# Expert layers of a 12-layer stack: the experts of the first 16 first keys worked densely from streamed blocks

## The chip, the cores and the metric

One core of one Trainium2 chip runs one program. The metric is the device time of a whole execution in microseconds. All data are float32; products that need float32 accuracy run either as one f32 matmul, which the trace shows as two MATMUL records, or as three products of split halves (fp32r, "hi" and "lo").

## What is computed

The reference is a stack of twelve layers over x of 256 tokens by 1024 columns: four gated FFNs, stick-breaking attention, latent attention, a state-space mixer, window attention with sinks, and twice the pair that this change touches, an expert layer and a gated embedding layer ("ple"). The expert layer, cut to what matters:

```python
h = rmsnorm(x, norm_g)                                   # 256 x 1024
q = (h @ q_w).reshape(T, 8, 2, 128)                      # 8 heads, two half queries
s = einsum('thcd,ckd->thck', q, sub_keys)                # scores on 128 first and 128 second keys
s1, i1 = top_k(s[:, :, 0], 16); s2, i2 = top_k(s[:, :, 1], 16)
best_s, best_pos = top_k(s1[..., :, None] + s2[..., None, :], 16)
idx  = the pair's i1 * 128 + i2                           # one of 16384 experts
gate = softmax(best_s)
a    = einsum('nd,nhkd->nhk', h, u[idx])                  # each expert: a row u and a row v of 1024
out  = einsum('nhk,nhkd->nd', gate * gelu(a), v[idx])
```

Every token picks 16 experts in each of 8 heads, 128 of 16384, and each picked expert is a row of u and a row of v, 8 KB together.

## The kernel before

Tokens lie on the 128 partitions, in two blocks (tb). A **unit** n (0 to 15) is one head of one block; a unit has 16 **picks**, worked in four **groups** of four (the last unit in eight smaller ones, FINE). For one pick GpSimd issues an indirect DMA that brings, for each of the 128 tokens, its row of `experts` (u and v side by side) into one of 11 buffers, `held`. VectorE makes the dot product of u with h (`dots`, L2723, one instruction of 1024 elements), ScalarE takes Gelu, multiplies by the gate and spreads the weight of each token on a diagonal (`weights`: L1903, L1905, L1912), and TensorE adds diagonal times v to the layer's sum in PSUM (`values`: L1300 and L1303, two halves of 512 columns). The last product of a pick frees its buffer (`expert_free`), and GpSimd waits for that before it issues the gather 11 picks later.

Each engine works through its own instruction list in order, and semaphores join the lists. The lists are written out by hand, group by group:

- TensorE, `peer`: 4 queries ahead (a query m is 8 products of a 128x128 weight block with 256 tokens, L1258; its key scores are L1288), then for each group: on every second group `key_scores(m - 1)` and `query(m)`, then `values`. `query_beside` says which query stands in which group; there are 16 of them, two for each head (both blocks at once).
- ScalarE: on those groups `scores(m - 1)` (PSUM to SBUF, L1884), then `weights`, then the copy of query m (L1892), which TensorE's key scores need.
- VectorE: `dots` of a group, and between the groups of unit n the search for unit n + 1: `gates` and `top_keys`, `top_pairs`, `experts_of` (L2665 to L2714 and L2179 to L2190), which yields the indices for the gathers.
- GpSimd: the gathers in order of picks, and some low parts (L401) of the ple layer's weight blocks.
- SP: the queue of the stream. All other weights come as blocks of 128x1024 (512 KB) from `stream`, four in a ring, and a load waits until the block four before it has been used (or split). Queries have places of their own.

In the last four units the ple layer begins beside the values (`ple_beside_values`).

The lines that set the order on TensorE:

```python
for n in range(UNITS):
    for group in range(len(groups_of(n))):
        m = query_beside(n, group)
        if m is not None:
            key_scores(m - 1)
            query(m)
        if m == SUBS - 1:
            key_scores(m)
        values(n, group)
        ple_beside_values(l, n, group)
```

Of the kernel before, what the change touches and what calls it, by code (L numbers as in the profile page):

```python
# [7 lines left out]
U32 = mybir.dt.uint32  # L8
# [33 lines left out]
RING = 4  # L42
LAYERS = ["ffn0", "sb", "ffn1", "ffn2", "mla", "ffn3", "ssm", "peer0", "ple0", "swa", "peer1", "ple1"]
# [3 lines left out]
         ("peer0_q", SUBS), ("ple0_proj", 2), ("ple0_gate", 8),  # L47
         ("swa_kv", 2), ("swa_q", 8), ("swa_out", 8),
         ("peer1_q", SUBS), ("ple1_proj", 2), ("ple1_gate", 8)]
# [29 lines left out]
LATE_BY_DVE = {AT[part] + k for part, ks in (("sb_out", (5, 7)), ("ple0_gate", (5, 7)), ("ple1_gate", (5, 7)),  # L79
# [64 lines left out]
EARLY_GATE = {(PH + 6, 2): 0, (PH + 6, 3): 1, (PH + 7, 0): 2, (PH + 7, 1): 3}  # L144
# [13 lines left out]
def build_program(nc, stream, experts, x_in, pos_in, cols_in, rows_in, out):  # L158
    n_blocks = AT["end"]
    ctx = ExitStack()  # L160
    with ctx:
# [149 lines left out]
        def peer_regions():  # L311
# [3 lines left out]
                       ("pk", (2, TOPK)), ("at", (TOPK,)), ("idx", (2, TOPK)), ("e", (2, TOPK)), ("sum", (1,)),  # L315
                       ("rc", (1,)), ("gate", (2, TOPK)), ("a", (2, TOPK)), ("g", (2, TOPK)), ("w", (2, TOPK)),
                       limit=HELD_AT)
            r["held"], _ = region(HELD_AT, HELD, EXPERT)
# [19 lines left out]
        h_for_queries = plain("h_for_queries", hT_at, KD, T)  # L338

# [43 lines left out]
        def make_hi(act, b, i=None, per_turn=0):  # L383

            wait_loaded(act, b, i, per_turn)
            if b in NEXT_IN_RING:
# [201 lines left out]
        def _(pe):  # L588
# [314 lines left out]
            def mla():  # L903
# [26 lines left out]
                latent_block(3, 0).then_inc(of("mla_first"), 1)  # L930
# [5 lines left out]
                for tb in range(TB):  # L936
# [15 lines left out]
                    if tb == 0:  # L952
                        last.then_inc(of("mla_q_done"), 1)
                for tb in range(TB):
# [10 lines left out]
                    if tb == 0:  # L965
                        last.then_inc(of("mla_kv_done"), 1)
# [127 lines left out]
            def ssm():  # L1094
# [47 lines left out]
                pe.wait_ge(of("ssm_ex"), 1)  # L1142
# [108 lines left out]
            def peer(l):  # L1251
# [41 lines left out]
                def values(n, group):  # L1293
                    tb = n // PH
                    pe.wait_ge(of("peer_diag"), group_count(l, n, group) + 1)
                    for k in range(*groups_of(n)[group]):
                        first, end = n % PH == 0 and k == 0, n % PH == PH - 1 and k == TOPK - 1
# [3 lines left out]
                        if tb == 1 and (first or end):  # L1301
                            lower.then_inc(y_ready, 1)
                        pe.matmul(ps[:, 2 * tb + 1, :], diag, v[:, HALF:D], start=first, stop=end)\  # L1303
                          .then_inc(of("expert_free"), 1)

# [24 lines left out]
            def ple_beside_values(l, n, group):  # L1330
# [11 lines left out]
                if (n, group) == (PH + 5, 0):  # L1342
                    pe.wait_ge(of("ple_pT"), l + 1)
                    project(1, 4).then_inc(of("ple_second"), 1)
                if (n, group) == (PH + 5, 1):
                    project(0, 0)
                if (n, group) == (PH + 5, 2):
# [1679 lines left out]
```

## Time and profile before

| | |
|---|---|
| median of 3 runs | 2742.69 us (2741.33 to 2744.24) |
| span of the profiled execution | 2739.2 us |
| TensorE busy (with modelled ends of matmuls) | 2461.3 us, 90% |
| VectorE busy | 1915.0 us, 70% |
| ScalarE busy | 1178.3 us, 43% |
| GpSimd busy | 855.8 us, 31% |
| gathers | 512, 536.90 MB |
| stream and the rest | 237.45 MB |

Busy shares are means over layers with different limits. How an expert layer stands has to be read from windows cut at its own ends, from who waits for whom there, and from the distances between starts in the timeline, since matmuls overlap their own ends.

### The profile page before, as it was taken

How to read it: one execution, taken by the hardware profiler on the slowest of the kernel's cores; microseconds unless marked ns; L12 is line 12 of the kernel's file. 1: busy time of each engine (PE TensorE's matmuls, PEld its weight loads, DVE VectorE, ACT ScalarE, POOL GpSimd, SP SyncE). 2: the span in 40 equal slices, each digit the busy share in tenths (PEclk: the TensorE clock that was granted, in tenths of full speed). 3: DMA queues.
4: the chain of work that ended last, by engine and by line, in shares of the span. 5: the costliest groups of instructions: out<-in, count | busy, mean ns of one | idle time of the engine just before them, and what ended most of it. 6: DMA issues, size and time to landing. Idle time of an engine off the chain costs nothing.

```text
span 2739.2 us, 32208 instructions
## 1 busy us (share of the span) xinstructions
PE 2461.3 (90%) x10416; PEld 1678.3 (61%) x10416; DVE 1915.0 (70%) x3841; ACT 1178.3 (43%) x2586; POOL 855.8 (31%) x700
## 2 busy tenths in 40 slices
PE   8999999999989999998998787789988998777688
PEld 7888788888778877986544333334765454333244
DVE  7885588888768875654676767666667676776675
ACT  4446744444564456563333333333453333323334
POOL 0005400000230026754333333444433333333442
PEclk9999999999999999999999889999999999999999
DMA  6654365556425553448999999999639999999996
GB/s 209 189 180 139 117 198 190 172 192 190 158 70 195 188 163 127 165 142 331 420 418 421 417 419 415 414 414 420 205 142 413 420 421 421 417 420 417 411 414 265
DMA packets 142240, 783.39 MB, mean 286 GB/s; under 512 B 15904, under 2 KB 16416, under 8 KB 76576
## 3 DMA queue, kind: packets, MB, share of 16 engines
q0 software_dynamic: 73728, 536.90, 47.4%
q1 hardware_dynamic: 65648, 237.45, 26.1%
q10 hardware_dynamic: 2736, 7.46, 0.9%
q8 instruction: 66, 1.08, 0.2%
q14 instruction: 62, 0.51, 0.1%
HBM read 780.69 MB, written 1.05 MB: 285 GB/s over the span
## 4 chain that ended last, share of the span: by engine, by line
PE 48%; DMA 22%; issue 9%; DVE 8%; ACT 7%; POOL 6%; another core or an unknown queue 0%; POOLq 0%; ACTq 0%; SPq 0%; DVEq 0%
DMA arena<-experts,arena 22%; PE ps L717 11%; PE ps L1300 6%; PE ps L1303 6%; PE ps L718 6%; PE ps L695 5%; PE ps L696 5%; PE ps L697 5%; POOL ring_lo L401 4%; DVE arena L2723 2%; ACT row L1912 2%; POOL arena L2840 1%; PE ps L1258 1%; ACT arena L1905 1%; ACT L1903 1%
## 5 line engine op out<-in xcount | busy, mean ns | idle before, releaser
L2723 DVE SCALAR_TENSOR_TENSOR arena<-arena,ps 128x1024 f32<-128x1024 f32 x512 | 616.4, 1219 | 370.3 <-DMA arena<-experts,arena 354.0
L1300 PE MATMUL ps<-arena,row 128*128 128x512 f32 x1024 | 568.3, 638 | 197.3 <-ACT row L1912 190.3
L2840 POOL DMA_INDIRECT arena<-experts,arena x512 | 485.3, 948 | 761.4 <-PE ps L1303 508.9
L1303 PE MATMUL ps<-arena,row 128*128 128x512 f32 x1024 | 549.7, 620 | 0.0
L717 PE MATMUL ps<-hT,ring_hi 128*128 128x512 f32 x1408 | 503.4, 400 | 2.9 <-DVE hT L2239 2.7
L394 ACT ACTIVATE ring_hi<-ring 128x1024 fp32r<-128x1024 f32 x408 | 429.8, 1058 | 172.4 <-PE ps L697 127.4
L1300 PEld LDWEIGHTS ps<-arena,row 128*128 128x128 f32 x1024 | 198.2, 202 | 474.5 <-ACT row L1912 259.5
L401 POOL TENSOR_TENSOR ring_lo<-ring,ring_hi 128x1024 fp32r<-128x1024 f32 x139 | 334.5, 2416 | 235.0 <-ACT ring_hi L394 212.7
L718 PE MATMUL ps<-hT,ring_lo 128*128 128x256 f32 x1408 | 395.9, 281 | 0.0
L1303 PEld LDWEIGHTS ps<-arena,row 128*128 128x128 f32 x1024 | 205.5, 201 | 266.4 <-issue 266.4
L401 DVE TENSOR_TENSOR ring_lo<-ring,ring_hi 128x1024 fp32r<-128x1024 f32 x269 | 324.1, 1228 | 18.3 <-ACT ring_hi L394 17.6
L717 PEld LDWEIGHTS ps<-hT,ring_hi 128*128 128x128 f32 x1408 | 265.3, 188 | 69.7 <-issue 3.1
L2817 POOL TENSOR_TENSOR rs<-ms,cols 128x1 f32<-128x1 f32 (+1 forms) x41 | 26.4, 645 | 842.2 <-DVE ms L2053 733.1
L718 PEld LDWEIGHTS ps<-hT,ring_lo 128*128 128x128 f32 x1408 | 266.7, 189 | 2.8
L1903 ACT ACTIVATE arena<-arena 128x4 f32<-128x4 f32 (+1 forms) x138 | 28.4, 206 | 533.2 <-DVE arena L2723 513.3
L1912 ACT ACTIVATE row<-cols,arena 128x128 f32<-128x128 f32 x512 | 164.6, 390 | 4.5
L695 PE MATMUL ps<-ring_hi,w 128*128 128x512 f32 x352 | 138.3, 393 | 3.0 <-DVE ring_lo L401 3.0
L1542 ACT ACTIVATE arena<-arena 128x256 f32<-128x256 f32 x88 | 36.9, 419 | 235.7 <-DVE arena L2280 235.7
L696 PE MATMUL ps<-ring_lo,w 128*128 128x512 f32 x352 | 137.9, 392 | 0.0
L697 PE MATMUL ps<-ring_hi,w 128*128 128x512 f32 x352 | 137.0, 389 | 0.0
L695 PE MATMUL ps<-hT,ring_hi 128*128 128x256 f32 (+1 forms) x392 | 114.1, 291 | 4.3 <-POOL ring_lo L401 2.4
L1905 ACT ACTIVATE arena<-arena 128x1 f32<-128x1 f32 x512 | 110.2, 284 | 4.5
(350 smaller groups left out, 3599.4 us busy)
## 6 DMA issues: line engine op xcount, KB each, us to landing
ring<-stream SPq DMA_DIRECT2D x424, 512.0 KB
arena<-experts,arena POOLq DMA_INDIRECT x512
row<-rows_in ACTq DMA_DIRECT2D x11, 512.0 KB, 5.2
arena<-stream SPq DMA_DIRECT2D x8, 512.0 KB, 5.8
queries_in_ring_hi<-stream SPq DMA_DIRECT2D x8, 512.0 KB
queries_in_w<-stream SPq DMA_DIRECT2D x4, 512.0 KB, 7.8
queries_in_h_lo<-stream SPq DMA_DIRECT2D x4, 512.0 KB, 5.3
x<-x_in SPq DMA_DIRECT2D x1, 1024.0 KB, 5.3
```

The lines of the kernel that those rows point to most:

```text
L394: act.activation(part(b)[0], raw(b), ACT.Copy).then_inc(hi_ready, 1)
L401: e.tensor_tensor(lo, raw(b), hi.bitcast(F32), ALU.subtract).then_inc(lo_ready[who], 1)
L695: pe.matmul(dst, a[0], b[0], start=start, stop=False)
L696: pe.matmul(dst, a[0], b[1], start=False, stop=False)
L697: return pe.matmul(dst, a[1], b[0], start=False, stop=stop)
L717: pe.matmul(ps[:, bank_at, :], hi, hT[:, :, k, :], start=k == 0, stop=False)
L718: last = pe.matmul(ps[:, bank_at, 0:T], lo, hT_hi[:, k, :], start=False, stop=k == KD - 1)
L1300: lower = pe.matmul(ps[:, 2 * tb, :], diag, v[:, 0:HALF], start=first, stop=end)
L1303: pe.matmul(ps[:, 2 * tb + 1, :], diag, v[:, HALF:D], start=first, stop=end)\
L1912: last = act.activation(R["diag"][:, k % (2 * GROUP), :], col("ident"), ACT.Copy, scale=R["w"][:, n % 2, k:k + 1])
L2723: last = dve.scalar_tensor_tensor(u, u, 1.0, h, ALU.mult, ALU.mult, accum_out=R["a"][:, n % 2, k:k + 1])
L2840: pool.indirect_dma_start(R["held"][:, g % HELD, :], None, experts, bass.IndirectOffsetOnAxis(ap=idx[:, n % 2, k:k + 1], axis=0))\
```

## The change

The keys are numbered 0 to 127, and an expert's index is first key times 128 plus second key. The experts whose first key is below `DENSE` = 16 are the first 2048 of the table. For these, u and v of the layer are laid into the stream: 16 blocks of u (transposed, one block for each first key) and 16 of v for each layer. The rest follows from that:

- **up**: `up(c)` multiplies block c of u with all of h (8 products of 256 tokens), one block in each group from (3, 0) to (6, 3); VectorE multiplies two blocks at a time with the inverse norm (`normed_dense`), ScalarE takes Gelu. The result is 128 second keys x 16 first keys x 256 tokens.
- **gates**: the picks of all 8 heads of a block are turned (`turned_picks`), VectorE compares them with iota (`first_keys_of`, `second_keys_of`), GpSimd multiplies the first-key comparison by the gate (`gated_first_keys`), and for each token one product of 128 picks x 128 second keys with 128 picks x 16 first keys gives the token's gates on all 2048 experts (`dense_gates`, 16 tokens in a "half", 16 halves, in units 8 to 10). VectorE multiplies them in (`dense_weights`).
- **down**: `down(c)` adds weights times block c of v to the same PSUM sums (4 products of 512 columns), from (10, 3) to (12, 3).
- **gathers**: an index whose first key is below 16 gets 2^20 added and falls out of the bounds check, so its row is not fetched (not in unit 0). Its gate in `values` is zero (`masked`), and the value products are made for all picks as before. From unit 2 on `dots` writes its elementwise result elsewhere.
- **order**: queries stand one in each group of units 0 to 2, and behind the values instead of before them. Searches are done two to a unit from unit 2 to 7 (`SEARCHED`). The ple layer's first steps move back by two to four groups; six low parts go from GpSimd to VectorE.
- Elsewhere some semaphores that one engine signals in order are merged into one (FFN, latent attention, state space).

```diff
-            m = FRONT + (len(EVEN) * n + group) // 2
-            return m if group % 2 == 0 and m < SUBS else None
+            m = FRONT + len(EVEN) * n + group
+            return m if m < SUBS else None
...
+SEARCHED = [[1], [2], [3, 4], [5, 6], [7, 8], [9, 10], [11, 12], [13, 14], [15]] + [[] for _ in range(UNITS - 9)]
+GATED_HALVES = {(8, 0): 1, (8, 1): 1, (8, 2): 1, (8, 3): 1, (9, 0): 2, (9, 1): 2,
+                (9, 2): 1, (9, 3): 2, (10, 0): 2, (10, 1): 2, (10, 2): 1}
+DENSE_VALUES = {(10, 3): 2, (11, 0): 2, (11, 1): 2, (11, 2): 2, (11, 3): 1, (12, 0): 2, (12, 1): 2, (12, 2): 2, (12, 3): 1}
+FIRST_KEYS = {(7, 2): 0, (9, 2): 1}
+TURNED_PICKS = {(7, 1): 0, (9, 1): 1}
...
                         if m is not None:
                             key_scores(m - 1)
+                        if (n, group) in TURNED_PICKS:
+                            turned_picks(TURNED_PICKS[n, group])
+                        values(n, group)
+                        if m is not None:
                             query(m)
                         if m == SUBS - 1:
                             key_scores(m)
-                        values(n, group)
+                        dense_beside_values(n, group)
...
+                def up(c):
+                    b, p = AT[f"peer{l}_u"] + c, c // 2
+                    if c % 2 == 0:
+                        if p < 2:
+                            pe.wait_ge(of("peer_s"), n0 + SUBS)
+                        else:
+                            pe.wait_ge(of("dense_by_dve"), by_dve(l, "normed", p - 2))
+                    wait_loaded(pe, b)
+                    for k in range(KD):
+                        last = pe.matmul(dense_bank(p)[:, (c % 2) * T:(c % 2 + 1) * T], raw(b)[:, k * P:(k + 1) * P],
+                                         parts_for_queries(k, slice(0, T)), start=k == 0, stop=k == KD - 1)
+                    last.then_inc(used, 1)
...
+                def dense_gates(i):
+                    pe.wait_ge(of("dense_by_pool"), HALVES // 2 * l + i // 2 + 1)
+                    pe.wait_ge(of("dense_by_dve"), by_dve(l, "second_keys", i))
...
+                    for t in range(TOPK):
+                        last = pe.matmul(gates_in(i)[:, t, :], second_keys[i % 2][:, t, :], first_keys[:, TOPK * i + t, :],
+                                         start=True, stop=True)
...
+                def down(c):
...
+                    for tb in range(TB):
+                        for half in range(2):
+                            last = pe.matmul(ps[:, 2 * tb + half, :], dense[:, c, tb * P:(tb + 1) * P],
+                                             raw(b)[:, half * HALF:(half + 1) * HALF],
+                                             start=False, stop=tb == 0 and c == DENSE - 1)
...
+                def normed_dense(p):
+                    if p == 0:
+                        dve.wait_ge(of("dense_by_act"), by_act(l, "inverse"))
+                    dve.wait_ge(used, AT[f"peer{l}_u"] + 2 * p + 2)
...
+                def dense_beside_dots(n, group):
+                    q = len(EVEN) * n + group - SUBS + FRONT
+                    if q >= 2 and q % 2 == 0 and q < DENSE + 2:
+                        normed_dense((q - 2) // 2)
+                    before = halves_of(*((n, group - 1) if group else (n - 1, len(EVEN) - 1)))
+                    for i in before:
+                        dense_weights(i)
+                    if (n, group) in FIRST_KEYS:
+                        first_keys_of(FIRST_KEYS[n, group])
+                    for i in halves_of(n, group):
+                        second_keys_of(i)
...
+                        dots(n, group)
+                        if group == 0:
+                            for searched in SEARCHED[n - 1] if n else [0]:
+                                gates(searched)
+                        dense_beside_dots(n, group)
+                        for _ in range((2, 1, 2, 1)[group] if len(SEARCHED[n]) > 1 else 1):
+                            if searches:
+                                part_of, searched = searches.pop(0)
+                                part_of(searched)
...
+                        if n:
+                            pool.indirect_dma_start(into, None, experts, rows, bounds_check=2 * KEYS * KEYS - 1,
+                                                    oob_is_err=False).then_inc(expert_landed[g % HELD], 16)
```

ScalarE's order within a group is not touched: `scores(m - 1)`, `weights`, the copy of query m.

## Rows read from the trace of the kernel before

**Rows 1.** The page's head.
```profile
span 2739.2 us, 32208 instructions
```
**Rows 2.** Windows: length, busy PE, PEld, DVE, ACT, POOL (instructions), PEclk, DMA share, GB/s.
```profile
1291.90:1403.50 111.60, 102.83 (x283) 52.97 (x284) 77.64 (x185) 37.48 (x123) 42.30 (x45) 0.97 1.01 421
1403.50:1602.50 199.00, 170.73 (x442) 82.82 (x442) 139.30 (x345) 66.65 (x215) 75.02 (x79) 0.95 1.01 418
1602.50:1801.50 199.00, 154.35 (x311) 64.02 (x310) 137.62 (x343) 61.20 (x190) 77.08 (x80) 0.91 1.01 414
1801.50:1927.40 125.90, 112.78 (x272) 52.02 (x270) 82.75 (x185) 47.71 (x144) 52.90 (x50) 0.95 0.99 411
2077.00:2712.70 635.70, 534.09 (x1305) 249.49 (x1305) 437.17 (x1056) 213.06 (x673) 248.29 (x253) 0.95 1.01 416
1572.70:1574.70 2.00, 2.00 (x3) 0.97 (x4) 1.48 (x5) 0.00 (x0) 0.00 (x0) 0.50 1.06 442
```
**Rows 3.** TensorE's waits in 1291.9 to 1927.4: us in total, times, longest.
```profile
PE ps L1300 <- ACT row L1912: 90.5, 42, 5.6
```
**Rows 4.** Timeline of TensorE: start, length; a value half, key scores, a query, values.
```profile
1304.90 1.02 PE L1303 MATMUL ps<-arena,row 128*128 128x512 f32 x2
1305.76 0.61 PE L1288 MATMUL ps<-arena,pick 128*128 128x128 f32 x4
1306.20 3.62 PE L1258 MATMUL ps<-h_for_queries,ring 128*128 128x256 f32 x16
1309.66 1.02 PE L1300 MATMUL ps<-arena,row 128*128 128x512 f32 x2
```
**Rows 5.** Timeline of TensorE in the state-space layer: f32 products of 64 columns.
```profile
1151.96 1.90 PE L1192 MATMUL ps<-arena 128*128 128x64 f32 x16
1153.69 0.65 PE L1194 MATMUL ps<-arena 128*128 128x256 f32 x2
```
**Rows 6.** Timeline of ScalarE beside rows 4, and a Gelu table load later.
```profile
1306.40 0.63 ACT L1884 ACTIVATE arena<-ps,rs 128x128 f32<-128x128 f32 x2 [8.26 <-PE ps L1288]
1306.92 0.20 ACT L1903 ACTIVATE arena<-arena 128x4 f32<-128x4 f32 x1
...
1308.05 1.28 ACT L1912 ACTIVATE row<-cols,arena 128x128 f32<-128x128 f32 x4
1309.86 0.38 ACT L1892 ACTIVATE pick<-ps 128x256 f32<-128x256 f32 x1 [0.54 <-issue]
...
1568.95 1.28 ACT L1903 ACT_TABLE_LOAD   x1 [7.57 <-DVE arena L2714]
```
**Rows 7.** Timeline of TensorE after an idle time: first value half, fourth.
```profile
1572.70 2.08 PE L1300 MATMUL ps<-arena,row 128*128 128x512 f32 x2 [3.97 <-ACT row L1912]
...
1577.82 1.02 PE L1303 MATMUL ps<-arena,row 128*128 128x512 f32 x2
```
**Rows 8.** Timeline of VectorE: where gates, dots, pairs and experts begin and end.
```profile
1568.24 0.17 DVE L2712 TENSOR_REDUCE arena<-arena 128x1 f32<-128x16 f32 x1
...
1571.65 1.22 DVE L2723 SCALAR_TENSOR_TENSOR arena<-arena,ps 128x1024 f32<-128x1024 f32 x1
...
1572.79 1.22 DVE L2723 SCALAR_TENSOR_TENSOR arena<-arena,ps 128x1024 f32<-128x1024 f32 x1
...
1578.17 0.42 DVE L2698 TENSOR_TENSOR arena<-arena 128x256 f32<-128x256 f32 x1
...
1581.09 1.21 DVE L2723 SCALAR_TENSOR_TENSOR arena<-arena,ps 128x1024 f32<-128x1024 f32 x1
...
1588.12 0.17 DVE L2179 TENSOR_SCALAR arena<-arena 128x16 uint32<-128x16 uint32 x1
...
1591.08 1.21 DVE L2723 SCALAR_TENSOR_TENSOR arena<-arena,ps 128x1024 f32<-128x1024 f32 x1
```
**Rows 9.** Groups of VectorE by shape: a comparison of 512 elements.
```profile
L2185 DVE TENSOR_TENSOR arena<-arena,cols 128x512 f32<-128x512 f32 x15 | 10.4, 692 | 0.5
```
**Rows 10.** The page's groups: a low part on GpSimd, 1024 elements.
```profile
L401 POOL TENSOR_TENSOR ring_lo<-ring,ring_hi 128x1024 fp32r<-128x1024 f32 x139 | 334.5, 2416 | 235.0 <-ACT ring_hi L394 212.7
```

More of the change, by code:

```diff
@@ L1296, in values @@
                     for k in range(*groups_of(n)[group]):
-                        first, end = n % PH == 0 and k == 0, n % PH == PH - 1 and k == TOPK - 1
+                        first, end = n % PH == 0 and k == 0, n == UNITS - 1 and k == TOPK - 1
                         v = R["held"][:, (PICKS * l + TOPK * n + k) % HELD, D:]
@@ L1300, in values @@
                         lower = pe.matmul(ps[:, 2 * tb, :], diag, v[:, 0:HALF], start=first, stop=end)
-                        if tb == 1 and (first or end):
+                        if end:
                             lower.then_inc(y_ready, 1)
@@ L1304, in values, with inverse_row @@
                           .then_inc(of("expert_free"), 1)
+                def inverse_row():
+                    pe.wait_ge(of("dense_by_act"), by_act(l, "spread"))
+                    for b in range(TB):
+                        last = pe.matmul(ps[:, 6, b * P:(b + 1) * P], col("ones"), R["spread"][:, b, :], start=True, stop=True)
+                    last.then_inc(of("dense_by_pe"), 1)
+                def up(c):
[10 more added lines that the diff above has]
+                    last.then_inc(used, 1)
@@ new lines, in down @@
+                def down(c):
+                    b = AT[f"peer{l}_v"] + c
+                    if c == 0:
+                        pe.wait_ge(of("dense_weights"), HALVES * (l + 1))
+                    wait_loaded(pe, b)
+                    for tb in range(TB):
[3 more added lines that the diff above has]
+                                             start=False, stop=tb == 0 and c == DENSE - 1)
+                        if tb == 0 and c == DENSE - 1:
+                            last.then_inc(y_ready, 1)
+                    last.then_inc(used, 1)
@@ new lines, in dense_beside_values @@
+                def dense_beside_values(n, group):
+                    c = dense_up(n, group)
+                    if c is not None:
+                        if c == 0:
+                            inverse_row()
+                        up(c)
+                    for i in halves_of(n, group):
+                        dense_gates(i)
+                    first = begun_at(DENSE_VALUES, (n, group))
+                    for c in range(first, first + DENSE_VALUES.get((n, group), 0)):
+                        down(c)
@@ L1914, in weights, with spread_inverse, inverse_row, gelu @@
                     last.then_inc(of("peer_diag"), 1)
+                def spread_inverse():
+                    act.wait_ge(of("peer_sp"), n0 + SUBS)
+                    for b in range(TB):
+                        last = act.activation(R["spread"][:, b, :], col("ident"), ACT.Copy, scale=rs[:, b:b + 1])
+                    last.then_inc(of("dense_by_act"), 1)
+                def inverse_row():
+                    act.wait_ge(of("dense_by_pe"), by_pe(l, "inverse"))
+                    act.activation(R["inverse"], ps[:, 6, 0:T], ACT.Copy).then_inc(of("dense_by_act"), 1)
+                def gelu(p):
+                    act.wait_ge(of("dense_by_dve"), by_dve(l, "normed", p))
+                    pair = dense[:, 2 * p:2 * p + 2, :]
+                    act.activation(pair, pair, ACT.Gelu).then_inc(of("dense_by_act"), 1)
+                def turned_picks(tb):
+                    act.wait_ge(of("dense_by_pe"), by_pe(l, "turned", tb))
+                    act.activation(R["turned"][:, tb], split(ps[:, 5 if tb else 2, 0:3 * P], 3, P), ACT.Copy)\
+                       .then_inc(of("dense_by_act"), 1)
+                def dense_beside_weights(n, group):
+                    q = len(EVEN) * n + group - SUBS + FRONT
+                    if q == 0:
+                        inverse_row()
+                    if q >= 3 and q % 2 and q < DENSE + 3:
+                        gelu((q - 3) // 2)
+                    if (n, group) in TURNED_PICKS:
+                        turned_picks(TURNED_PICKS[n, group])
                 second_high_parts()
```

266 lines of the change are left out of this document (184 added, 82 removed).

## Prediction

> **What bounds the kernel now.** The span of the profiled execution is 2739.2 us [rows 1]; the median of the runs shown is 2742.69, so what is worked out on the span gets 3.5 us added. I took the page's 40 slices first, saw DMA near full only in the two stretches of the expert layers, and then asked for windows cut at the first and last value product of each layer [rows 2]: 1291.9 to 1927.4 in layer 0 (635.5 us) and 2077.0 to 2712.7 in layer 1 (635.7 us). The four windows of layer 0 hold 48, 80, 80 and 48 picks; the reader should see a DMA share of 0.99 to 1.01 and 411 to 421 GB/s in all of them. The waits say the same: TensorE waited 90.5 us for ScalarE's diagonals [rows 3], which follow VectorE's dots and so the gathers. So one expert row pair of 1.05 MB costs 2.49 us, a unit of 16 picks 39.8 us, and any byte saved there looks like time saved. But TensorE is the next limit and not far off: 541 us of busy time in 635.5 (the first four windows of rows 2 together), with modelled ends in it. Its real pace is in the timeline: one half of a pick's value product every 0.86 us [rows 4], so four picks take 6.86 us of the 9.95 that their gathers take. All that TensorE has left per layer is 635 - 64 x 6.86 = 196 us, of which the 12 queries beside the values (3.46 us each, and 0.44 for the key scores [rows 4]) take 47 and the work of the next layer some 20.
>
> **The change, part by part.**
> Bytes removed: counting in the reference on these inputs, 4022 and 4068 rows of units 1 to 15 have a first key below 16, 66.3 MB at 8 KB a row. Bytes added: 64 blocks of 0.524 MB, 33.6 MB. Net 32.7 MB, 78 us at 417 GB/s, if bytes still decided.
>
> TensorE, added per layer. Up: 16 blocks of the very shape of a query, 16 x 3.46 = 55 us. Down: 16 x 4 products of 512 columns at 0.86, 55 us. Gates: 256 products with 128 weight columns and 16 moving ones. The trace has none. From below: if only moving columns cost, a query's record of 256 columns at 0.216 us gives 0.014 each, 7 us in all. From above: key scores with 128 columns, 4 records in 0.44 us, 56 us. The nearest row has 64 columns: 16 records from 1151.96 to 1153.69, 0.108 each [rows 5]. I take 0.108, thus 0.216 a token, 3.46 for a half of 16 tokens, 55 us in all. (The Trainium skill, TensorE: Matmul & The Clock Gate, section LDWEIGHTS, says that a weight load takes its number of stationary columns divided by 1.2, in ns; for 128 that is 107, and the row agrees. The same page's formula for an isolated gap, section Back-to-back issue gap, goes by moving columns; by it the 512 records would cost some 5 us and TensorE's sum be 624, not 674, an estimate; the page says itself that it under-counts at few columns.) Sum: 165 us added to about 506, 671 and with transposes 674, against 635 before. No value product is taken away: every pick keeps its two halves, with weight zero. That alone turns a saving of bytes into a loss.
>
> Then the order. I call w TensorE's work in a group and follow who waits.
>
> Units 0 to 2 (12 groups). Before, on every second group, TensorE did key scores, query, values, and the query (3.46) hid ScalarE's scores and weights. Now each group does key scores of m-1, values, query m. ScalarE's queue has scores(m-1) ahead of weights of the group, and scores(m-1) need the query that TensorE made at the end of the group before. So a chain stands bare in each group: drain and copy 0.20 + 0.38 (1309.66 to 1310.24), 0.05, key scores to scores 0.64, scores 0.52, Gelu to last diagonal 2.41 (1306.92 to 1309.33), 0.05: 4.25 us [rows 4, 6]. Group = 6.86 + 3.46 + 4.25 = 14.6. Twelve: 175; two Gelu table reloads of 1.28 [rows 6]: 178; and before (3,0) the spread of rs, an Exp load and exponentials, and two units' gates ahead of that Gelu: about 5.3: 183. All of VectorE and the gathers hide under it.
>
> The clock. After an idle of 3.97 us TensorE is granted 0.50, the 1.2 GHz level, and takes 5.12 us (1572.70 to 1577.82) for three halves that take 2.57 at 2.4 GHz [rows 7, 2]. Gaps of 3 to 4 us are what the new chains make, so each may cost 0 to 2.55; the mean grant of 0.91 in the third window says not each one, and I take 1.5. Units 0 to 2: 183 + 12 x 1.5 = 201, before 111.6.
>
> Units 3 to 7. The searches go two to a unit. VectorE's pieces [rows 8]: gates plus keys 3.41 (by its small instructions I give gates 0.5 of it, 0.8 with the new mask, and keys 2.9), pairs 2.92, experts 2.96, a dot 1.14 (four 4.7 with the new wait for the group before). normed_dense(p) stands in VectorE's queue after dots of q = 2p+2 and waits for up(2p+1), which TensorE does after the values of q-1. From its end: 0.2 + 0.69 (512 elements, [rows 9]) + keys and pairs 5.8 + dots 4.7 + ScalarE 2.6 = 14.0 us to the next group's values, while TensorE has values and up, 10.3. So 3.7 idle, plus clock 1.5: a pair of groups 25.8 instead of 19.9. Two free groups 21.2, seven pairs 181, gates of two units three times 1.6: 5; unit 7 is VectorE's (14.0 + 1.6, then 8.7, 12.8 with first_keys, 7.7): 44. Together 250, before 199.
>
> Units 8 to 12. A 2048-element comparison is four of the 0.69 rows less their fixed part, 2.3 us [rows 9]; 16 + 2 a layer, 41 us that VectorE hides except in unit 8, where search and comparison chain with TensorE as above (13.1 against 10.3, 11.7 a group): 48 with clock. Units 9 and 10: 27.4 + 7 and 5 halves of 3.46, 2 downs of 3.43: 51.6 each, and 3 for the wait of turned_picks(1) on dense_weights. Units 11 and 12: 27.4 + 7 x 3.43 = 51.4 each. Sum 257, before 199.
>
> Units 13 to 15: gathers bound again, 16 x 2.49 x 0.87 = 34.6 a unit, with the stream's blocks and the tail 108, before 126.
>
> Costed at nothing, with their cover: GpSimd's multiply of 512 elements (half of a low part's 2.42 us [rows 10]) and a bounds check per gather, both under its idle time, as 79 instructions took 75.02 us of 199 [rows 2], 0.95 each of the 2.49 between gathers; they would show if an issue passed 2.5 us. SP's loads of u and v wait for blocks used, 1.26 us each at 417 GB/s against 3.4 us or more between uses; uncovered, 16 x 1.26 x 2. Low parts moved from GpSimd to VectorE, at most 6 x 2.42, lie in units 13 to 15 where VectorE waits for rows. The merged semaphores in the FFN layers only join counts of one queue. Block 0's sum, mean and power come later, in the same waits.
>
> Layer: 201 + 250 + 257 + 108 = 816 against 635.5, +180.5; two layers +361; 2739.2 + 361 + 3.5 = 3104, say 3100.
>
> **The rivals.**
> A, bytes decide: 2742.7 - 78 = 2665. It needs TensorE's 674 us under 635 - 39 = 596, so values or ups cheaper than rows 4, from the point where w falls under 9.3 us a group. DMA at 1.01 speaks for it, the pace of 0.86 against it. This is the one on the other side of zero.
> B, TensorE alone: the chains are hidden because VectorE and ScalarE run ahead. Units 0 to 2: 3 x 27.4 + 47 = 129; 3 to 6: 4 x 41.3 = 165; 7: 35; 8 to 12: 137 + 110 = 247; 13 to 15: 108. That is 684, +48 a layer, 2840. For it: VectorE is busy for 437 of 635.5 us [rows 2]. Against it: both chains close through a queue's own order, which being ahead can't cure.
> C, dearer: the lower clock takes every stall in full and a checked gather or comparison beside GpSimd costs more: 3104 + 44 x 1.05 = 3150 and beyond, to 3300.
> D, the skipped rows are fetched all the same: 676 us of DMA a layer, under 816, so no change to my number; with B it would still be 2840.
>
> **How the numbers follow.** Forecast 70%, its own range 3030 (no clock loss) to 3160 (2.55 each time). B, or a part of the chains hidden down to 2950: 15%. C above 3200: 8%. A: 5%. No change 2%. If gates cost their low bound, VectorE's chain takes over in units 8 to 10 and 25 us a layer go, to 2980 with no clock loss. The range of 8 in 10 is 2950 to 3200. 0.2% (5.5 us) is what a measurement of this kernel tells from none: faster 0.05, same 0.02, slower 0.93.
>
> **What would show it.** Value products with 14 to 17 us from group to group in units 0 to 2, TensorE idle behind ScalarE's diagonals once for each; in units 3 to 6 idle of some 4 us on every second group and VectorE waiting for L1258's like; gates at 0.108 a record; DMA share near 0.75 over the layer, 1.0 only at its end. Wrong if DMA stays at 1.0 throughout, or if group distances in units 0 to 2 stay near 11.

## The result, and the profile after

The changed kernel takes 3178.91 us (median of 4 runs, 3177.32 to 3180.35) against 2742.01 (4 runs); the ratio is 1.1599, with a 95% interval of 1.1582 to 1.1615. That is slower by 437 us. The prediction said 3100 in 2950 to 3200, and slower with 0.93.

First the page of the changed kernel, the rows that answer to [rows 1] and to the busy times and gathers of the table before.

```profile
span 3177.7 us, 37104 instructions
...
PE 2896.0 (91%) x12228; PEld 2004.9 (63%) x12228; DVE 2027.2 (64%) x3999; ACT 1157.0 (36%) x2588; POOL 878.2 (28%) x704
...
q0 software_dynamic: 73728, 470.66, 39.8%
q1 hardware_dynamic: 74864, 271.00, 25.1%
...
PE 69%; DVE 12%; issue 7%; ACT 6%; POOL 4%; DMA 2%; POOLq 0%; ACTq 0%; SPq 0%; DVEq 0%
```

The reader is to see that the gathers moved 66 MB less (470.66 for 536.90), the stream 34 MB more (271.00 for 237.45), as counted. The last line is the chain that ended last: 69% TensorE and 2% DMA, where it was 48% and 22% before. The saving of bytes came, and in this kernel it was worth nothing: DMA is hardly on that chain any more.

Windows of the changed kernel, layer 0, cut by the count of value records (16 for each group of four picks) at the starts of units 0, 3, 8, 13 and at the end. The columns are those of [rows 2].

```profile
1285.60:1492.50 206.90, 155.80 (x432) 85.84 (x432) 92.41 (x253) 47.91 (x156) 47.24 (x48) 0.87 0.66 241
1492.50:1749.20 256.70, 221.43 (x584) 119.39 (x585) 191.23 (x545) 65.92 (x210) 80.00 (x81) 0.88 0.83 311
1749.20:2043.60 294.40, 284.60 (x964) 166.04 (x962) 149.46 (x239) 50.53 (x186) 91.95 (x88) 0.87 0.78 286
2043.60:2147.10 103.50, 99.27 (x248) 47.56 (x248) 60.42 (x100) 38.52 (x122) 41.63 (x39) 0.96 0.89 355
```

The DMA share is 0.66 to 0.89 where it was 0.99 to 1.01, and the granted clock 0.87 to 0.88 in the first three windows and 0.96 in the last, where it was 0.91 to 0.97. The same cut on the kernel before gives 120.8, 199.8, 205.4 and 109.5 us. The windows of [rows 2] were cut some 9 us early: they do not hold 48 picks in the first, as the prediction said, and the 111.6 and 126 that it compared with should have been 120.8 and 109.5. The layer's sum is not touched by that. Layer 1 after the change is 861.8 us long, layer 0 861.5, before 635.5 and 635.4. So 452 us were added in the layers, and 14 us less lie outside them. The kernels below that are made from the code before with one edit in the expert layer have 12 to 16 us less there too, so these are not the work of the change's edits outside the layers. Ten of the 14 can be placed: shortly before the first values of each layer of the kernel before, TensorE waited 4.67 and 5.33 us for ScalarE's copy of a query, and e9_before_skip shows no wait there. The first of the two:

```profile
1277.22 0.78 PE L1272 MATMUL ps<-arena,pick 128*128 128x128 f32 x2 [4.67 <-ACT pick L1874]
```

Why ScalarE was late there stays open. When a kernel is compared with the kernel before, the layers say what an edit did in them; the medians hold these 14 us as well.

### The profile page after: what moved, and what is told of

It is laid out like the page before. It is cut to its first block, busy times and chain, and to the rows that moved or that the text cites. A ratio compares the mean times of both kernels' runs of the same rounds, so it can differ in the third digit from the quotient of the medians.

```text
span 3177.7 us, 37104 instructions
## 1 busy us (share of the span) xinstructions
PE 2896.0 (91%) x12228; PEld 2004.9 (63%) x12228; DVE 2027.2 (64%) x3999; ACT 1157.0 (36%) x2588; POOL 878.2 (28%) x704
## 3 DMA queue, kind: packets, MB, share of 16 engines
q0 software_dynamic: 73728, 470.66, 39.8%
q1 hardware_dynamic: 74864, 271.00, 25.1%
## 4 chain that ended last, share of the span: by engine, by line
PE 69%; DVE 12%; issue 7%; ACT 6%; POOL 4%; DMA 2%; POOLq 0%; ACTq 0%; SPq 0%; DVEq 0%
PE ps L1371 14%; PE ps L1374 12%; PE ps L788 9%; PE ps L789 5%; PE ps L766 5%; PE ps L767 5%; PE ps L768 5%; PE ps L1416 4%; POOL ring_lo L472 4%; PE ps L1427 3%; PE ps L1329 3%; PE ps L1392 2%; DMA arena<-experts,arena 2%; ACT row L2056 2%; DVE arena L2910 2%
## 5 line engine op out<-in xcount | busy, mean ns | idle before, releaser
L1371 PE MATMUL ps<-arena,row 128*128 128x512 f32 x1024 | 614.7, 686 | 198.1 <-ACT row L2056 197.9
L2910 DVE SCALAR_TENSOR_TENSOR arena<-arena,ps 128x1024 f32<-128x1024 f32 x376 | 448.5, 1217 | 247.5 <-DMA arena<-experts,arena 242.5
L1374 PE MATMUL ps<-arena,row 128*128 128x512 f32 x1024 | 578.6, 649 | 0.0
L1371 PEld LDWEIGHTS ps<-arena,row 128*128 128x128 f32 x1024 | 214.6, 217 | 447.6 <-issue 228.6
L1374 PEld LDWEIGHTS ps<-arena,row 128*128 128x128 f32 x1024 | 219.7, 215 | 294.9 <-issue 294.9
L472 POOL TENSOR_TENSOR ring_lo<-ring,ring_hi 128x1024 fp32r<-128x1024 f32 x127 | 306.0, 2420 | 233.3 <-ACT ring_hi L465 211.5
L472 DVE TENSOR_TENSOR ring_lo<-ring,ring_hi 128x1024 fp32r<-128x1024 f32 x281 | 338.7, 1228 | 18.4 <-ACT ring_hi L465 17.4
L1416 PEld LDWEIGHTS ps<-first_keys,second_keys 128*128 128x128 f32 x1024 | 150.6, 236 | 10.5 <-issue 10.5
L1416 PE MATMUL ps<-first_keys,second_keys 128*128 128x16 f32 x1024 | 148.7, 296 | 0.0
L2910 DVE SCALAR_TENSOR_TENSOR queries_in_h_lo<-arena,ps 128x1024 f32<-128x1024 f32 x96 | 113.6, 1216 | 27.2 <-DMA arena<-experts,arena 27.2
```

The lines of the kernel that those rows point to most:

```text
L472: e.tensor_tensor(lo, raw(b), hi.bitcast(F32), ALU.subtract).then_inc(lo_ready[who], 1)
L1371: lower = pe.matmul(ps[:, 2 * tb, :], diag, v[:, 0:HALF], start=first, stop=end)
L1416: last = pe.matmul(gates_in(i)[:, t, :], second_keys[i % 2][:, t, :], first_keys[:, TOPK * i + t, :], start=True, stop=True)
L2910: last = dve.scalar_tensor_tensor(unread(n, k, u), u, 1.0, h, ALU.mult, ALU.mult, accum_out=R["a"][:, n % 2, k:k + 1])
```

## The experiments

Stage times of layer 0, all counted alike, from the profiled execution of each kernel; the median is that of its runs (e13_before_skip_all has one run):

| kernel | median us | units 0-2 | 3-7 | 8-12 | 13-15 | layer |
|---|---|---|---|---|---|---|
| before | 2742 | 120.8 | 199.8 | 205.4 | 109.5 | 635.4 |
| changed | 3179 | 206.9 | 256.7 | 294.4 | 103.5 | 861.5 |
| e1_query_first | 3013 | 129.9 | 245.0 | 294.4 | 103.6 | 772.9 |
| e2_gates_apart | 3193 | 206.5 | 256.7 | 301.6 | 103.7 | 868.5 |
| e3_filler | 3151 | 191.5 | 254.7 | 294.4 | 104.1 | 844.8 |
| e4_norm_later | 3080 | 206.8 | 209.4 | 290.4 | 103.7 | 810.3 |
| e5_before_new_queries | 2894 | 207.9 | 196.3 | 205.0 | 109.5 | 718.6 |
| e6_gates_mid | 3153 | 206.7 | 256.7 | 281.2 | 104.1 | 848.7 |
| e8_gates_wide | 3119 | 206.8 | 256.7 | 265.1 | 105.0 | 833.6 |
| e9_before_skip | 2673 | 119.9 | 189.6 | 194.5 | 103.8 | 607.9 |
| e10_gates_64_columns | 3126 | 206.4 | 256.7 | 267.9 | 104.3 | 835.3 |
| e11_together | 2869 | 129.9 | 204.6 | 264.3 | 104.2 | 703.0 |
| e12_together_sum_later | 2852 | 129.9 | 206.8 | 259.4 | 105.6 | 701.6 |
| e13_before_skip_all | 2499 | 115.0 | 160.6 | 142.9 | 99.2 | 517.7 |

**Queries ahead of the values again.**

```diff
                             turned_picks(TURNED_PICKS[n, group])
-                        values(n, group)
                         if m is not None:
                             query(m)
                         if m == SUBS - 1:
                             key_scores(m)
+                        values(n, group)
```

> The changed kernel, with query m ahead of the values again (still one in each group of units 0 to 2). If the chain query copy, key scores, scores, weights stands bare because the query comes behind the values, then the query of 3.46 us hides it: a group of units 0 to 2 falls from 17.2 us to 10.8 to 11.2, the stage from 207 to 130 to 140 us, and the kernel to about 3040. If the groups are long for another reason (rows landing late, VectorE), the stage stays above 190 us and the time at 3179.

3012.6 us, ratio 1.099 (1.0972 to 1.1008). One group of the changed kernel in the timeline of TensorE:

```profile
1311.47 3.62 PE L1329 MATMUL ps<-h_for_queries,ring 128*128 128x256 f32 x16
1315.56 0.71 PE L1359 MATMUL ps<-arena,pick 128*128 128x128 f32 x4 [0.47 <-ACT pick L2036]
1319.28 2.07 PE L1371 MATMUL ps<-arena,row 128*128 128x512 f32 x2 [3.00 <-ACT row L2056]
1321.14 1.92 PE L1374 MATMUL ps<-arena,row 128*128 128x512 f32 x2
```

And ScalarE beside it, the same chain as in [rows 6]:

```profile
1315.12 0.38 ACT L2036 ACTIVATE pick<-ps 128x256 f32<-128x256 f32 x1 [12.37 <-PE ps L1329]
1316.31 0.62 ACT L2028 ACTIVATE arena<-ps,rs 128x128 f32<-128x128 f32 x2 [0.80 <-PE ps L1359]
1316.83 0.20 ACT L2047 ACTIVATE arena<-arena 128x4 f32<-128x4 f32 x1
...
1317.95 1.28 ACT L2056 ACTIVATE row<-cols,arena 128x128 f32<-128x128 f32 x4
```

The query ends about 1314.93, the values begin at 1319.28: 4.35 us bare, 4.25 predicted, and then a half takes 1.86 us (1319.28 to 1321.14) for 0.86 at full clock. The kernel's time is 27 us under the expected 3040: the stage is at the low end of 130 to 140, and units 3 to 7 gave another 12 us in layer 0. With the query ahead most groups take 10.8 or 10.9 us, and TensorE in that stage goes from 155.80 busy in 206.90 to 126.81 in 129.90 at clock 1.00:

```profile
1284.80:1414.70 129.90, 126.81 (x416) 74.95 (x416) 92.47 (x253) 47.80 (x157) 46.59 (x47) 1.00 0.94 366
```

**The change's handling of the queries alone, on the kernel before.**

```diff
-            m = FRONT + (len(EVEN) * n + group) // 2
-            return m if group % 2 == 0 and m < SUBS else None
+            m = FRONT + len(EVEN) * n + group
+            return m if m < SUBS else None
...
                             key_scores(m - 1)
+                        values(n, group)
+                        if m is not None:
                             query(m)
                         if m == SUBS - 1:
                             key_scores(m)
-                        values(n, group)
```

> The kernel before with one thing of the change: a query in every group of units 0 to 2, behind the values. By the bare chain the stage takes 207 us instead of 121 and the rest, bound by gathers, is as before: 2742 + 2 x 86 = about 2914. Rival: the harm needs the dense layer's other loads on ScalarE and VectorE, and alone it is below 30 us, 2770.

2893.8 us, ratio 1.056 (1.0542 to 1.0577): 207.9 us in units 0 to 2 with none of the dense work. Its waits there are the changed kernel's: in the first fence the changed kernel, in the second this one.

```profile
PE ps L1371 <- ACT row L2056: 43.0, 12, 5.5
```

```profile
PE ps L1300 <- ACT row L1913: 42.7, 12, 5.3
```

So a good third of the loss is there with the new places of the queries alone, one in each group and behind the values: 83 of the 226 us that the change adds to layer 0 (152 of 437 in the medians, with the 14 us outside the layers in both). That the order is the part that costs is shown by the run before this one, which kept one query in each group and got 166 us back.

**Clock: work put into the idle time.**

```diff
                             key_scores(m - 1)
+                            unread_products(11)
```

> The changed kernel with 11 products of 128x128x128 f32 that nobody reads, put behind the key scores of units 0 to 2, in the 3.0 us in which TensorE is idle. If the idle time costs clock (0.50 granted for 3 to 5 us behind it), the groups fall from 17.2 us to about 15 and the kernel to about 3135, although TensorE does more. If the clock does not fall for that idle time, or if narrow products do not hold it, the groups stay at 17 and the time at 3179 or above.

3151.1 us, ratio 1.1497. More work, 28 us less time. Its timeline:

```profile
1315.80 2.62 PE L739 MATMUL ps<-cols 128*128 128x128 f32 x22
1318.97 1.12 PE L1371 MATMUL ps<-arena,row 128*128 128x512 f32 x2 [0.55 <-ACT row L2057]
1319.94 1.02 PE L1374 MATMUL ps<-arena,row 128*128 128x512 f32 x2
```

Six of the twelve groups fell to 14.8 us, the bare chain's period without the clock (14.6 predicted); the others stood at 16.2 and more. The mean granted clock of the stage rose from 0.87 to 0.96:

```profile
1287.70:1479.20 191.50, 167.39 (x674) 106.95 (x674) 92.31 (x253) 47.97 (x156) 47.39 (x48) 0.96 0.71 260
```

The theory holds, and the gain is 28 us of the 44 expected.

**normed_dense one group later.** In the changed kernel `normed_dense(p)` waits for an `up` that TensorE does in the very group before, and everything behind it in VectorE's queue, the next dots among it, waits too; TensorE's next values need these dots (through ScalarE). Two queues that hold each other in this way are called a lock here.

```diff
-                    if q >= 2 and q % 2 == 0 and q < DENSE + 2:
-                        normed_dense((q - 2) // 2)
+                    if q >= 3 and q % 2 and q < DENSE + 3:
+                        normed_dense((q - 3) // 2)
```

> The changed kernel with normed_dense(p) one group later in VectorE's queue (behind the dots of q = 2p+3). If the lock of units 3 to 6 is VectorE's wait for up(2p+1) of the group just before, it is gone: two groups fall from 27.2 us to about 21, units 3 to 7 from 257 to about 220 us, the kernel to about 3105. Rival: VectorE's double searches bound these units by themselves (19 to 20 us of work in two groups) and the wait only stands where idle time was anyway: 250 us or more, 3165 to 3179.

3080.4 us, ratio 1.1242 (1.1223 to 1.126). VectorE's wait in units 3 to 7 of the changed kernel, and the stage with the edit:

```profile
DVE dense L2932 <- PE ps L1392: 59.4, 8, 9.5
```

```profile
1491.20:1700.60 209.40, 200.72 (x583) 112.45 (x584) 191.59 (x545) 66.02 (x211) 81.75 (x81) 0.97 0.96 380
```

Two groups went from 27.2 to 20.6 us, 10.3 each, which is TensorE's values and up with nothing between. VectorE's wait for `up` is gone: in this stage it waits for nothing but rows, 11.7 us in all. VectorE is busy for the same 191 us in both; it was not the bound, only its order was. The stage gave 47 us, more than the 37 expected. The execution in the trace is the fastest of the five (3062.8 us, the others 3080 to 3084), so its stage times add up to 117 us of gain where the medians show 98.

**The gates: why do two halves in a row cost 14 us?** A group with two halves of gates takes up to 20.8 us, 14 more than its values. Stage 8 to 12 was 37 us a layer longer than predicted. The changed kernel's timeline shows where:

```profile
1791.14 3.64 PE L1416 MATMUL ps<-first_keys,second_keys 128*128 128x16 f32 x32
...
1803.28 11.25 PE L1416 MATMUL ps<-first_keys,second_keys 128*128 128x16 f32 x64
```

32 records take 3.5 us from their start to that of the values behind them, 0.109 each as predicted, but 64 take 11.25 (the five such runs of layer 0 take 8.86 to 11.25). The granted clock in them; 0.87 is the mean of a stretch in which it fell from 1.00 to 0.50:

```profile
1803.30:1806.90 3.60, 3.60 (x31) 3.60 (x29) 0.90 (x2) 2.33 (x9) 1.19 (x2) 0.87 0.96 373
1806.90:1814.50 7.60, 7.60 (x36) 7.51 (x36) 0.42 (x1) 0.00 (x0) 0.00 (x0) 0.50 0.60 243
```

TensorE has no gap in this time, and the clock still falls to 0.50, the 1.2 GHz level, and stays there into the values that follow. It can fall behind a lone half as well. Behind the 32 records of 1791.14, with no gap either, two value halves took 1.58 and 1.71 us for 0.86:

```profile
1795.70:1799.00 3.30, 3.30 (x6) 1.22 (x5) 3.30 (x2) 0.00 (x0) 0.84 (x1) 0.50 0.97 405
```

Three runs ask why. The theory is that a run of these narrow products, 16 moving columns each, loses the clock; the rival is that the second half is slow by its own data or its PSUM bank.

First, a half ahead of the values and one behind (`dense_gates` of all but the last half put before `values`):

```diff
-                    for i in halves_of(n, group):
+                    for i in halves_of(n, group)[-1:]:
                         dense_gates(i)
...
+                        for i in halves_of(n, group)[:-1]:
+                            dense_gates(i)
                         values(n, group)
```

> The changed kernel; where a group has two halves of gates, the first is done ahead of the values and the second behind them. The same products, none less. [...] Groups with two halves fall from 20.8 us to about 14, units 8 to 12 from 294 to about 260 us, the kernel to about 3110. Rival: the second half is slow for its own data or for its PSUM bank (banks 4 and 5 alternate): the halves keep 7 us wherever they stand, and the time stays at 3179.

3193.3 us, ratio 1.1648: worse. The edit did not part them: the half ahead of the values stood right behind the last half of the group before, and TensorE waited 2.8 us between them for its second keys. It tells nothing between the two theories, only that I had not looked across the group's border.

Second, the first half in the middle of the values, between the products of one pick and the next:

```diff
                           .then_inc(of("expert_free"), 1)
+                        if k % GROUP == 1:
+                            for i in halves_of(n, group)[:-1]:
+                                dense_gates(i)
...
-                    for i in halves_of(n, group):
+                    for i in halves_of(n, group)[-1:]:
                         dense_gates(i)
```

> The changed kernel; where a group has two halves of gates, the first stands in the middle of the values (behind the second pick) and the second behind them, so that 3.4 us of wide products part any two halves; the run before, with halves at both ends of a group, left two halves side by side across the group's border with 2.8 us of idle time between. Theory (a long run of 16-column products loses the clock): every half costs 3.5 us, groups with two halves go from 20.8 to about 14 us, units 8 to 12 from 294 to about 260 us, the kernel to about 3110. Rival (the second half is slow by its data or its bank): no change, 3179.

3153.1 us, ratio 1.1504. Twelve of the 16 halves of layer 0 now took 3.5 us and none took 7, so the rival (slow by data or by bank) is out. But the five groups with two halves still took 15.6 to 21.4 us: with 3.4 us of wide products between the halves the clock still fell, now often in the values. The gain is 26 us of 69 expected.

Third, four times the moving columns:

```diff
-                        last = pe.matmul(gates_in(i)[:, t, :], second_keys[i % 2][:, t, :], first_keys[:, TOPK * i + t, :],
-                                         start=True, stop=True)
+                        w_, at_ = t % 4, TOPK * i + min(t, 12)
+                        last = pe.matmul(gates_in(i)[:, 4 * w_:4 * w_ + 4, :], second_keys[i % 2][:, t, :],
+                                         first_keys[:, at_:at_ + 4, :], start=True, stop=True)
```

> The changed kernel, each gate product with 64 moving columns instead of 16 (the columns of four tokens, written over each other's place, so that the gates of the dense experts are not the reference's); the same 128-column weights, the same order, two halves in a row. If the weight load sets the pace, a record stays at 0.108 us. If it is the narrowness that loses the clock, the clock now holds, 64 records in a row take 7 us instead of 11.2, units 8 to 12 fall to about 260 us and the kernel to about 3110. If a run of weight loads itself loses the clock, whatever its columns, 11.2 us and 3179 stay.

3119.0 us, ratio 1.1379 (1.136 to 1.1398). Four times the columns, and 64 records take 7.25 us instead of 11.25, at full clock:

```profile
1801.22 7.25 PE L1417 MATMUL ps<-first_keys,second_keys 128*128 128x64 f32 x64
```

```profile
1801.20:1804.80 3.60, 3.60 (x34) 3.58 (x33) 2.73 (x6) 0.81 (x5) 1.31 (x2) 1.00 0.95 346
1804.80:1808.40 3.60, 3.60 (x33) 3.54 (x32) 0.42 (x1) 1.53 (x6) 0.00 (x0) 1.00 1.01 419
```

The record costs 0.11 us with 16 and with 64 columns, so the moving columns do not pace it; the clock fell with the narrow moving side and not with the wide one, and the rest of the records is alike. The values behind the lone half keep the clock too, at the same place in the list:

```profile
1794.50:1801.00 6.50, 6.50 (x16) 2.90 (x16) 6.50 (x6) 0.00 (x0) 2.94 (x3) 1.00 0.97 388
```

The same width can be had with the computation whole, since a token's product may write over places whose own products come later:

```diff
-                        last = pe.matmul(gates_in(i)[:, t, :], second_keys[i % 2][:, t, :], first_keys[:, TOPK * i + t, :],
-                                         start=True, stop=True)
+                        end_ = min(t + 4, TOPK)
+                        last = pe.matmul(gates_in(i)[:, t:end_, :], second_keys[i % 2][:, t, :],
+                                         first_keys[:, TOPK * i + t:TOPK * i + end_, :], start=True, stop=True)
```

> The changed kernel with the whole computation kept: each token's gate product also moves the columns of the next three tokens, into the next three tokens' places, which are written over by their own products later. So 13 of 16 products have 64 moving columns and the result is as before. If only the width of the moving side holds the clock, the time is that of the run with 64 columns, about 3120 against 3179, with units 8 to 12 near 265 us.

3125.5 us, ratio 1.1406: 53 us less with the same result. The mean granted clock of units 8 to 12 is 0.97 for 0.87.

**What the bytes are worth.** The kernel before, with `past` added to the index and the bounds check as in the change, and no dense work:

```diff
+                if n:
+                    dve.tensor_scalar(R["past"][:, ks], R["pk"][:, 0, ks], 16.0, float(1 << 20), ALU.is_lt, ALU.mult)
...
+                    return dve.scalar_tensor_tensor(R["idx"].bitcast(U32)[:, n % 2, ks], R["past"][:, ks],
+                                                    float(KEYS * KEYS * l), R["at"][:, ks], ALU.add, ALU.add)
...
+                            pool.indirect_dma_start(into, None, experts, rows, bounds_check=2 * KEYS * KEYS - 1,
+                                                    oob_is_err=False).then_inc(expert_landed[g % HELD], 16)
```

> The kernel before with the rows of the first 16 first keys left out of the gathers and nothing put in their place (these picks are computed on what the buffer held before, so the output is not the reference's). 66.3 MB fewer at 417 GB/s: if a skipped row costs nothing and bytes bound the layer, 2742 - 159 + a little for TensorE's queries, about 2595. If a skipped row takes the queue as long as a fetched one, 2742.

2673.5 us, ratio 0.9758 (0.9742 to 0.9774): 68 us, not 147. Of these, some 13 lie outside the layers, as in every kernel here but the one before; the layers gave 27.5 and 28.3 us, about 56. In the same window, before and with rows skipped (two kernels, two fences):

```profile
1420.00:1800.00 380.00, 308.05 (x701) 137.72 (x700) 262.99 (x645) 121.00 (x383) 145.24 (x152) 0.93 1.01 416
```

```profile
1420.00:1800.00 380.00, 318.55 (x731) 142.81 (x731) 278.82 (x697) 131.73 (x414) 164.87 (x162) 0.93 0.96 384
```

The queues are still busy for 0.96 of the time and move 384 GB/s instead of 416. To see whether a skipped row costs, all were skipped:

```diff
-                    dve.tensor_scalar(R["past"][:, ks], R["pk"][:, 0, ks], 16.0, float(1 << 20), ALU.is_lt, ALU.mult)
+                    dve.tensor_scalar(R["past"][:, ks], R["pk"][:, 0, ks], 128.0, float(1 << 20), ALU.is_lt, ALU.mult)
```

> The kernel before with all rows of units 1 to 15 left out of the gathers (picks computed on what unit 0 left in the buffers; the output is not the reference's). The run that skipped 8090 rows took 124 us of queue time off, 77% of their share, and left as many packets. If a skipped row still costs the queues 23% of a fetched one, a gather takes about 0.6 us of DMA time, far under TensorE's 1.72, and the DMA share falls to about 0.35; TensorE then bounds the layer: 64 x 6.86 + 47 + 20 and stalls, some 520 us, the kernel about 2510. If skipped rows are free, the share is near 0.05 and the time the same.

2499.4 us in a single run. The page's queue row:

```profile
q0 software_dynamic: 73728, 33.83, 4.5%
```

4.5% of 2497.5 us is 112 us; the 33.83 MB that unit 0 fetched take 82 of them at the rate of before (47.4% of 2739.2 us for 536.90 MB), so by this estimate 61,440 skipped rows took about 30 us, 0.5 ns each where a fetched one takes 20 (1298 us for 65,536). A skipped row by itself is nearly free, and my 23% is wrong. Why a mixture of fetched and skipped rows moves at 384 GB/s is open; that a gather is as late as its slowest queue, with unequal rows on the queues, would fit the share of 0.96, and was not tried.

This run shows too what TensorE and the chains alone need: 517.7 us for a layer, the prediction's 506 for values, queries and the next layer's work and a little idle time.

**All three mends together** (the edits of e1_query_first, e4_norm_later and e10_gates_64_columns in one), and then block 0's sum one group later:

```diff
+                        if (n, group) == (PH + 5, 0):
+                            add_piece(layer, in_banks, 0)
...
-                    if n == PH + 4:
-                        add_piece(layer, in_banks, 0)
...
```

> The changed kernel with the three mends together: queries ahead of the values, normed_dense one group later, gates moved 64 columns wide. Stages should add up from the single runs: 130 + 209 + 262 + 104 = 705 us a layer against 635.5 before, so 2742 + 139 - 12 (the layer starts 6 us earlier) = about 2870. By this the change stays slower than the kernel before even with every wait that was found taken away, since TensorE's own work (674 us in the prediction) fills the layer. Rival: with the waits gone the fewer bytes pay, and it comes out below 2742.

> As the run before, and block 0's sum is added to x one group later, behind the dots of (13, 0), so that VectorE does not hold these dots until the last down product. The group from (12, 3) falls from 17.7 to 13.7 us: 4 us a layer, 2862 where the run before has 2870. Rival: the dots were late for their rows and nothing moves.

2869.3 us, ratio 1.0473 (1.0456 to 1.0491), and 2852.2, ratio 1.04 (1.0382 to 1.0417). The whole layer of the first:

```profile
1287.10:1990.10 703.00, 673.65 (x2210) 376.67 (x2210) 492.49 (x1134) 202.86 (x674) 267.03 (x255) 0.99 0.92 357
```

TensorE is busy for 674 us of 703 at clock 0.99. In the second, VectorE no longer waits for the last down product ahead of these dots; in the changed kernel it had:

```profile
2034.74 1.22 DVE L2410 TENSOR_TENSOR x<-x,ps 128x1024 f32<-128x1024 f32 x1 [26.04 <-PE ps L1427]
```

The group from (12, 3) fell from 17.7 to 10.3 us, more than to the 13.7 expected, and unit 12 from 58.9 to 51.5; 17 us of time in all, where 8 were expected. No version tried that does the dense work beats the kernel before. But of the 226 us that the change added to layer 0, 160 are gone in this one with all products kept: by the rows above they were order and clock, and 66 us are left.

## Why the prediction was right, point by point

The time lies in the range of 8 in 10, but above the forecast's own range of 3030 to 3160, between it and rival C. The layers were 45.5 us longer than forecast each (861.5 for 816), 91 us in all; that the total missed 3104 by only 75 is in part luck, for 14 us fell away outside the layers and 3.5 us had been added to the span where 1.2 are right.

- **TensorE is the next limit, 674 us of work against 635.** Shown: with the three mends the layer takes 703 us, TensorE busy for 673.65, and the kernel stays 4.7% slower than before (4.0% with the sum later).
- **Units 0 to 2, 201 us.** Measured 206.9 and 206.5. The chain of 4.25 us was 4.35; the order alone, on the kernel before, gives 207.9.
- **Clock after idle time, 1.5 us of 0 to 2.55.** In units 0 to 2 nine groups stood at 16.5 to 17.4 us against 14.8 without the loss, so about 2.2 a group: low, inside its bounds. The fourth group of a unit took 17.2 us with and without unread products in its idle time (the last one 19.2), so no clock loss shows there, and the sum, some 20 us for 18, came out. In units 3 to 6 the value was further off, 3.2 us for a pair of groups.
- **Units 3 to 7, 250 us.** Measured 256.7. The lock was where it was put, and the edit that undoes it takes 47 us. A pair of groups took 27.2 us where 25.8 stood: 3.4 of wait for 3.7, and 3.2 of clock for 1.5.
- **Gates at 0.108 a record, 55 us.** The size failed, and with it units 8 to 12: 257 predicted, 294.4 measured, 37 of the 45.5 us that a layer was longer than forecast. The wider products take 29 of these 37 away. The price was read from a row of 64 columns, and the record costs as much with 16; but in 64 such records in a row the clock fell, and then they and the first values behind them go at half the rate. The term that was mis-sized is "3.46 for a half": it is 3.5 for the first and 5.4 to 7.8 for a second one in a row. The clock term was put on idle time alone.
- **Block 0's sum "in the same waits", at nothing.** It cost 7.4 us in the layer, most of the rest of the 37: VectorE held the dots of (13, 0) until the last down product, and unit 12 took 58.9 us where 51.4 stood; one group later it takes 51.5.
- **Units 13 to 15, 108 us.** Measured 103.5 and 104.2, but "gathers bound again" was not so: the DMA share there is 0.89, not the 1.0 that was named as a sign, and with nearly all rows skipped (e13_before_skip_all) the stage still takes 99.2 us.
- **Costed at nothing.** A checked gather's issue took 1.01 us for 0.95, and the multiply on GpSimd 1.07 to 2.23 us for 512 elements; neither shows in a wait. The merged semaphores show nowhere: the time outside the layers is within 2 us of that of e5_before_new_queries and e9_before_skip, which lack them.
- **Rival A, bytes decide.** Refuted, and its price was too high as well: the skipped rows alone give about 56 us in the two layers, where 147 were expected, on a layer whose TensorE has room.
- **Rival B, TensorE alone, 2840.** e12_together_sum_later comes near it, 2852 and 702 us a layer for 684: fair as a floor, wrong as a forecast, since queue orders are not cured by running ahead.
- **Rival D.** Skipped rows are not fetched: the gathers moved 470.66 MB.

## What to carry to other kernels

Before saving bytes on a bound queue, add up the next engine's work from starts in the timeline, not from busy shares: here its values left 196 us of a layer, 67 of them were taken already, and it was given 165 more. That sum alone foretells only the smaller part of this loss: 66 of 226 us a layer are left when order and clock are mended. Then walk each engine's list across group borders and ask, for every wait, whether what it waits for was issued one group ago (a lock) or two (free): moving one step of VectorE by one group gave 98 us, and swapping two calls on TensorE 166. And price a new small operation by what it does to those behind it, not by its own duration alone.

## What the runs showed of the hardware

- A run of f32 products with 128 weight columns and 16 moving ones, with no gap between records, was seen to lose the granted clock on the way, from 1.00 to 0.50 (64 records in 11.25 us). With 64 moving columns the same run stays at 1.00 (7.25 us). Both take 0.11 us a record at full clock. Behind a lone run of 32 narrow records the values went at 0.50 for 3.3 us, behind 32 wide ones at 1.00.
- An indirect DMA whose rows are all out of bounds costs the queues about 0.5 ns a row (an estimate: 30 us for 61,440), a fetched row of 8 KB 20 ns (1298 us for 65,536); but with one row in eight skipped the queues' rate fell from 416 to 384 GB/s.
- Unread products in TensorE's idle time made the kernel 28 us faster; the granted clock of the stage rose from 0.87 to 0.96.
